# Splitting streamed weights in 128x1024 pieces in place of 128x512, in a kernel of 86 weight blocks

## What is computed

```python
h = rmsnorm(x, g_pre[i])
proj = h @ w_in[i]
qkv, z_a, b_raw, a_raw, glu_in, z_b, gate_logits = jnp.split(proj, _split_points(), axis=-1)
qkv = jax.nn.silu(causal_depthwise_conv(qkv, w_conv_qkv[i]))          # 4 taps
o_a = gated_delta_chunked(q, k, v, g_log, beta)                       # 16 heads
y_a = o_a @ w_br_a[i]
u = causal_depthwise_conv(jax.nn.glu(glu_in), w_dw[i]) + b_dw[i]      # 31 taps
u = jax.nn.silu(layernorm(u, ln_g[i], ln_b[i])) * jax.nn.silu(z_b)
y_b = u @ w_br_b[i]
mixed = (gate_a * y_a + gate_b * y_b) @ w_out[i]
```

## Time and profile before

| | |
|---|---|
| median of 3 runs | 2382.02 us |
| span of the profiled execution | 2380.3 us |
| TensorE products busy | 2285.8 us, 96% |
| VectorE busy | 1580.1 us, 66% |
| ScalarE busy | 1267.6 us, 53% |
| GpSimd busy | 195.4 us, 8% |
| low parts (L401) | 1376 instructions, 941.2 us |
| high parts (L395) | 1376 instructions, 839.7 us |

### The profile page before, as it was taken

One profiled execution on the slowest core, in us unless ns is written; L12 is line 12 of the kernel. 1 busy time (PEld: TensorE's weight loads), 2 busy tenths in 40 slices (PEclk: granted clock), 3 DMA queues, 4 the chain that ended last, 5 costly groups with the idle time before them and its releaser, 6 DMA issues.

```text
span 2380.3 us, 32496 instructions
## 1 busy us (share of the span) xinstructions
PE 2285.8 (96%) x10970; PEld 1869.3 (79%) x10970; DVE 1580.1 (66%) x2901; ACT 1267.6 (53%) x2513; POOL 195.4 (8%) x357
## 2 busy tenths in 40 slices
PE   6999999999999899899999999999999989999997
PEld 5788878788777777777888888788888868888885
DVE  4766666666699999987555556465366664456665
ACT  4555555555566666657444555455345445555542
POOL 0001010010123232220000000000000000000000
PEclk9999999999999999999999999999999999999998
DMA  6634343343456666654665656556555545654462
GB/s 202 177 107 125 106 118 111 106 123 107 120 154 166 186 176 169 165 189 161 236 204 189 237 197 204 198 182 208 150 191 172 200 143 181 194 177 130 153 212 89
DMA packets 400631, 393.47 MB, mean 165 GB/s; under 512 B 15296, under 2 KB 284624, under 8 KB 398992
## 3 DMA queue, kind: packets, MB, share of 16 engines
q1 hardware_dynamic: 395968, 369.57, 50.4%
q0 software_dynamic: 4272, 20.45, 2.6%
q10 hardware_dynamic: 288, 2.10, 0.2%
HBM read 387.85 MB, written 4.21 MB: 165 GB/s over the span
## 4 chain that ended last, share of the span: by engine, by line
PE 77%; DVE 13%; issue 6%; ACT 3%; DMA 1%; SPq 1%; DVEq 0%; POOL 0%; ACTq 0%; POOLq 0%
PE pair L423 20%; PE pair L421 20%; PE pair L422 20%; DVE acc L846 5%; DVE w_lo L401 3%; PE RA L623 2%; PE RB L635 2%; PE RB L633 2%; PE RA L1214 1%; PE QA L1199 1%; PE QA L479 1%; PE RB L627 1%; ACT w_hi L395 1%; ACT bth L774 1%; PE QA L759 0%
## 5 line engine op out<-in xcount | busy, mean ns | idle before, releaser
L401 DVE TENSOR_TENSOR w_lo<-raw,w_hi 128x512 fp32r<-128x512 f32 x1376 | 941.2, 697 | 443.5 <-ACT w_hi L395 443.1
L395 ACT ACTIVATE w_hi<-raw 128x512 fp32r<-128x512 f32 x1376 | 839.7, 628 | 489.5 <-PE pair L423 479.6
L421 PE MATMUL pair<-w_hi,in_hi 128*128 128x512 f32 x2368 | 981.7, 415 | 14.8 <-DVE w_lo L401 7.4
L423 PE MATMUL pair<-w_hi,in_lo 128*128 128x512 f32 x2368 | 930.9, 393 | 0.0
L422 PE MATMUL pair<-w_lo,in_hi 128*128 128x512 f32 x2368 | 928.2, 392 | 0.0
L421 PEld LDWEIGHTS pair<-w_hi,in_hi 128*128 128x128 f32 x2368 | 448.9, 190 | 102.8 <-DVE w_lo L401 9.5
L423 PEld LDWEIGHTS pair<-w_hi,in_lo 128*128 128x128 f32 x2368 | 447.3, 189 | 95.9
L422 PEld LDWEIGHTS pair<-w_lo,in_hi 128*128 128x128 f32 x2368 | 449.3, 190 | 83.5 <-issue 4.8
L846 DVE SCALAR_TENSOR_TENSOR acc<-upad,cwl,acc 128x256 f32<-128x256 f32 x336 | 187.3, 594 | 0.0
L667 ACT ACTIVATE tri<-RB 128x512 f32<-128x512 f32 x96 | 54.1, 563 | 145.7 <-PE RB L635 145.7
L715 DVE TENSOR_TENSOR xm<-RA,const 128x256 f32<-128x256 f32 x96 | 40.8, 425 | 76.8 <-PE RA L623 76.8
(11 more groups left out here) (370 smaller groups left out, 2106.1 us busy)
## 6 DMA issues: line engine op xcount, KB each, us to landing
raw<-in_w_in_dram SPq DMA_DIRECT2D x512, 256.0 KB, 3.6
raw<-in_w_in_dram SPq DMA_DIRECT2D x80, 1024.0 KB, 5.2
raw<-in_w_out_dram SPq DMA_DIRECT2D x48, 1024.0 KB, 5.0
raw<-in_w_kv_shared_dram SPq DMA_DIRECT2D x24, 1024.0 KB, 5.0
raw<-in_w_br_a_dram SPq DMA_DIRECT2D x16, 1024.0 KB, 5.1
raw<-in_w_br_b_dram SPq DMA_DIRECT2D x16, 1024.0 KB, 5.0
raw<-in_w_mem_kv_dram SPq DMA_DIRECT2D x16, 1024.0 KB, 4.9
raw<-in_w_ple_gate_dram SPq DMA_DIRECT2D x16, 1024.0 KB, 5.0
```

The source lines that it names most:

```text
L395: act.activation(w_hi[:, u % 2, q % UK], raw[:, u, q % UK], ACT.Copy).then_inc(hi_ready[u], 1)
L401: dve.tensor_tensor(w_lo[:, u % 2, q % UK], raw[:, u, q % UK], w_hi[:, u % 2, q % UK].bitcast(F32), ALU.subtract)\
L421: pe.matmul(o, xh, wh, start=(q == 0), stop=False)
L423: mm = pe.matmul(o, xl, wh, start=False, stop=(q == KC - 1))
```

## The change

High and low parts are made for two chunks at a time, on 128x1024, 688 instructions each in place of 1376. A pair is indexed by r = 0 to 7; three pairs are split ahead in place of six chunks. TensorE waits once for each pair. In the even lists ScalarE makes a pair ahead of `between` at hs 0, 4, 8, ... and VectorE after it at hs 1, 5, 9, ... In the lists for heads ScalarE makes its pair *after* `between`, at hs 0, 4, 9, 12, 16, 20, 24, 28, and VectorE at 3, 6, 10, 13, 18, 21, 25, 29. Cut to its core:

```diff
-AHEAD = 6
+PAIRS = KC // 2
+UP = UK // 2
+AHEAD = 3
@@ load_unit, load_heads
-        reach(sp, lo_ready[u], UK * blk)
+        reach(sp, lo_ready[u], UP * blk)
@@ hi_piece, lo_piece
+    def pair_of(x, r):
+
+        u, c = r // UP, r % UP
+        return x[:, u % x.shape[1], 2 * c:2 * c + 2].rearrange("p k n -> p (k n)")
+
-        if q == 2 * UK - 1:
+        if r == UP * 2 - 1:
             reach(act, psum_ready, blk)
-        elif q < 2 * UK:
-            reach(act, chunk_used, (KC - 1) * blk - (2 * UK - 2 - q))
+        elif r < 2 * UP:
+            reach(act, chunk_used, (KC - 1) * blk + 2 * r - 5)
         else:
-            reach(act, chunk_used, (KC - 1) * blk + q - 2 * UK + 1)
-        act.activation(w_hi[:, u % 2, q % UK], raw[:, u, q % UK], ACT.Copy).then_inc(hi_ready[u], 1)
+            reach(act, chunk_used, (KC - 1) * blk + 2 * (r - 2 * UP) + 2)
+        act.activation(pair_of(w_hi, r), pair_of(raw, r), ACT.Copy).then_inc(hi_ready[u], 1)
...
+        dve.wait_ge(hi_ready[u], UP * blk + r % UP + 1)
+        dve.tensor_tensor(pair_of(w_lo, r), pair_of(raw, r), pair_of(w_hi, r).bitcast(F32), ALU.subtract)\
            .then_inc(lo_ready[u], 1)
@@ pe_block
-            pe.wait_ge(lo_ready[u], UK * blk + q % UK + 1)
+            if q % 2 == 0:
+                pe.wait_ge(lo_ready[u], UP * blk + q % UK // 2 + 1)
@@ act_block, dve_block
+    HI_EVENLY, LO_EVENLY = tuple(range(0, 2 * KC, 4)), tuple(range(1, 2 * KC, 4))
+    HI_BESIDE_HEADS, LO_BESIDE_HEADS = (0, 4, 9, 12, 16, 20, 24, 28), (3, 6, 10, 13, 18, 21, 25, 29)
+
+    def act_block(act, blk, between=None, pieces_at=HI_EVENLY):
+        for hs in range(2 * KC):
+            first = pieces_at is HI_EVENLY
+            if between and not first:
+                between(hs)
+            if hs in pieces_at:
+                b, r = ahead(blk, pieces_at.index(hs))
+                if not isinstance(b, int) or b < BLK_END:
+                    hi_piece(act, b, r)
+            if between and first:
+                between(hs)
```

More of the change, by code:

```diff
@@ L381, in loads, with hi_piece, lo_piece, ahead @@
         return 64 * blk + 64
-    def hi_piece(act, blk, q):
-        u = q // UK
-        if q % UK == 0:
+    def pair_of(x, r):
+        u, c = r // UP, r % UP
+        return x[:, u % x.shape[1], 2 * c:2 * c + 2].rearrange("p k n -> p (k n)")
+    def hi_piece(act, blk, r):
+        u = r // UP
+        if r % UP == 0:
             act.wait_ge(w_loaded[u], loads(blk))
-        if q == 2 * UK - 1:
+        if r == UP * 2 - 1:
             reach(act, psum_ready, blk)
-        elif q < 2 * UK:
-            reach(act, chunk_used, (KC - 1) * blk - (2 * UK - 2 - q))
-        else:
-            reach(act, chunk_used, (KC - 1) * blk + q - 2 * UK + 1)
-        act.activation(w_hi[:, u % 2, q % UK], raw[:, u, q % UK], ACT.Copy).then_inc(hi_ready[u], 1)
[L397 to L401, removed]
+        elif r < 2 * UP:
+            reach(act, chunk_used, (KC - 1) * blk + 2 * r - 5)
+        else:
+            reach(act, chunk_used, (KC - 1) * blk + 2 * (r - 2 * UP) + 2)
+        act.activation(pair_of(w_hi, r), pair_of(raw, r), ACT.Copy).then_inc(hi_ready[u], 1)
+    def lo_piece(dve, blk, r):
+        u = r // UP
+        dve.wait_ge(hi_ready[u], UP * blk + r % UP + 1)
+        dve.tensor_tensor(pair_of(w_lo, r), pair_of(raw, r), pair_of(w_hi, r).bitcast(F32), ALU.subtract)\
            .then_inc(lo_ready[u], 1)
[L404 to L408, removed]
+    def ahead(blk, r):
+        if r + AHEAD < PAIRS:
+            return blk, r + AHEAD
+        return blk + 1, r + AHEAD - PAIRS
     def pe_block(pe, blk, parity, hi, lo, between=None):
@@ L429, in pe_block, with dve_block @@
                     between(2 * q + tile)
[L431 to L444, removed]
+    HI_EVENLY, LO_EVENLY = tuple(range(0, 2 * KC, 4)), tuple(range(1, 2 * KC, 4))
[11 more added lines that the diff above has]
+                between(hs)
+    def dve_block(dve, blk, between=None, pieces_after=LO_EVENLY):
         for hs in range(2 * KC):
@@ L448, in dve_block @@
             if hs in pieces_after:
-                b, p = ahead(blk, pieces_after.index(hs), 1)
+                b, r = ahead(blk, pieces_after.index(hs))
                 if not isinstance(b, int) or b < BLK_END:
-                    lo_piece(dve, b, p)
+                    lo_piece(dve, b, r)
     def keys_pe(pe, h, par, hs):
@@ L1893, in _ @@
         act_block(act, 1, beside([(keys, 0, 0)]))
-        heads = lambda h, i: act_block(act, h + i, beside([(rule, h + (i - 2), i), (keys, h + (i - 1), 1 - i)]))
+        heads = lambda h, i: act_block(act, h + i, beside([(rule, h + (i - 2), i), (keys, h + (i - 1), 1 - i)]), HI_BESIDE_HEADS)
         heads(2, 0)
@@ L1923, in _ @@
         dve_block(dve, 1, beside([(keys, 0, 0)]))
-        heads = lambda h, i: dve_block(dve, h + i, beside([(rule, h + (i - 2), i), (keys, h + (i - 1), 1 - i)]), BESIDE_HEADS)
+        heads = lambda h, i: dve_block(dve, h + i, beside([(rule, h + (i - 2), i), (keys, h + (i - 1), 1 - i)]), LO_BESIDE_HEADS)
         heads(2, 0)
```

## The result

The changed kernel takes 2403.12 us (median of 4 runs, 2402.38 to 2404.49) where the kernel before, run beside it, takes 2382.91 (2381.13 to 2384.28): 1.0082 times as long, 95% interval 1.0069 to 1.0094. That is 20.2 us slower; the forecast was 15.8 slower. Its profiled execution has a span of 2400.6 us, 20.3 more than the earlier trace rows.

What follows compares the result with a forecast made beforehand. TensorE was taken to bound heads and tail, VectorE the groups. Heads +24.6, groups -9.8 and start +1 give +15.8 us on a span of 2380.3, as a median 2397.8 us; 8 in 10 range 2384 to 2409.

Steps and rivals of the forecast that it cites:

- What bounds the kernel: TensorE bounds heads and tail, where shorter splits gain nothing; VectorE bounds the groups, where a cheaper split can pay.
- The heads' stalls: Blocks 2 to 15: low pairs waiting for high pairs behind `tri` delay `xm` by 0.88 us twice a block, +24.6 us.
- the gain at the start of the rule: Heads: VectorE has no piece at half-steps 31 and 1 any more, which can only help; counted 0.
- The groups: VectorE's rounds get 0.7 us shorter with pairs, -9.8 us over 14 rounds; bounds 0 and -27.3.
- The length of a round: Groups: a block takes about 24.3 us, with TensorE's waits near 1.4.
- TensorE's waits cover that: Groups: TensorE's waits, 2.1 us mean, cover the 0.7 us saved a round, so 14 rounds give -9.8.
- Rival (b): Heads stall, but groups gain nothing, as pairs bound to used chunks hold VectorE at more half-steps: 2407.6 us; chance 0.13.
- rival (c): Stalls in the heads make TensorE's clock fall there as in the groups, 8.6 us more: 2406.4 us; chance 0.08.
- The start: Block 1: TensorE's first product is behind one high and one low part, which grow by 0.95 us; taken as +1.
- The tail: Pairs are made in time on two half-idle engines: 0, between -2 and +2 us.
- the evictions behind a high pair in the groups: Groups: ScalarE's evictions of half-step 0 stand behind a high pair, but are covered by 1.1 us.
- blocks 16 to 18: Forecast 0; blocks 16 and 17 use the even list, with the high pair ahead of `tri`, so no stall.

Runs made afterwards that it cites:

- three experiments on order: Changed kernel, heads only: high pairs at half-steps 8 and 11, 2379.46 us; low pairs at 11 and 14, 2378.01; only the high pair of 9 moved to 8, 2390.95.
- Counted in chunks: Pairs everywhere, heads' high pairs at half-steps 8 and 11, each pair raising its counter by two: 2384.15 us, against 2379.46 for the same counted in pairs.
- the late list: Groups' low pairs at half-steps 1, 5, 11, 15, 19, 22, 25, 29, not 1, 5, 9, 13, 17, 21, 25, 29; alone in the changed kernel: 2394.79 us.
- the best version: Pairs in blocks 2 to 32 only, heads' high pairs at half-steps 8 and 11, groups' low pairs at 11, 15, 19, 22: 2368.64 us, ratio 0.9937.
- the kernel with single pieces at late places: The 2368.64 us kernel with each pair of the groups taken apart into two 128x512 pieces at the same queue place; heads keep pairs: 2378.41 us.
- the run with one late piece: Kernel before, one 512 piece per head in the changed order: high part behind `tri` at half-step 9, low part ahead of `xm` at 10: 2382.84 us.
- the three kernels with pairs at the late places: Groups' low pairs at half-steps 11, 15, 19, 22: pairs in blocks 2 to 32 only, 2368.64 us; in the changed kernel, 2394.79; with all orders mended, 2369.38.

## Why the prediction was right, and where it was off

**The range.** The measured 2403.12 us lies in the 8 in 10 range (2384 to 2409) and, by 0.1, outside the forecast's own (2392 to 2403).

**What bounds the kernel.** Right in the main: the tail gained nothing from the smaller work on VectorE, the groups did. The heads have a gain too, 3.3 us without the stalls, but by a place in the queue, as follows.

**The heads' stalls.** The mechanism and its size were right: `xm` 0.88 us late at half-steps 11 and 14 and nowhere else (block 11, half-step by half-step), 2.72 us from `tri` where the working had 2.71, the load's wait 1.13 where it had about 1.1, and the clock at 1.00. The three experiments on order confirm it from both engines and one stall at a time. What was mis-sized is the gain at the start of the rule, which was counted at 0 for want of a row: each block gets 0.24 us back there, so it takes 38.77 us, not 39.0, and the term is 14 x (1.76 - 0.24) = 21.3, against 24.6. In block 11 the first `xm` starts 1.94 us into the block in place of 2.19, and half-step 3 is 0.24 us earlier, with pairs counted either way: VectorE has no piece ahead of it at half-step 1 any more. Counted in chunks, about 0.08 of it is lost again at the hand-over ahead of `r` shown above.

**The groups.** The length of a round was right: 24.05 to 24.5 us without a fall, where 24.3 was forecast. But the rounds before averaged 24.91 over these 14 blocks (348.7 / 14), falls and all, and those of after 24.3 without what two falls cost ((342.8 - 2.4) / 14), so that 0.6 a round or 8.3 us is what the pairs saved, near the 9.8. The step that failed is the one behind it, "TensorE's waits cover that". It was worked out as if the falls of the clock stayed as harmless as they were; they were harmless because VectorE never waited for a high part that itself waited for a used chunk. A pair needs the later of its two chunks, and with that VectorE's round hangs on TensorE's: two falls left 1.2 us each. -8.3 + 2.4 = -5.9. Rival (b), that pairs bound to used chunks hold VectorE at more places, was half true, and through the clock; rival (c) looked for falls in the heads, where there are none, and missed that those in the groups would begin to count. The fall in block 33 (38.84 before, 40.64 after) is the +1.5 of that stretch; no step had it, and as another kernel's trace has it with the late list and two have not, part of it may be chance.

**The start.** +1.0 came as forecast: the first product of block 1 is at 59.56 in place of 58.6. A single trace could not have shown it, for this place varies by over a microsecond between traces (58.5 to 60.1 us in the six with single pieces there, 59.6 to 61.0 in the eight with pairs); the means are 59.1 and 60.1. It was given back within block 1, which waits later for other things: near 0 at block 2.

**The tail.** 2.7 against a bound of 2, and named nowhere: the prediction priced the evictions behind a high pair in the groups, and not in the tail, where the products of nine blocks wait for them.

The errors partly cancel: -3.4 in the heads, +3.9 in the groups, +4.2 in the tail and around block 33, -1.2 at the start and +0.9 in blocks 16 to 18 add, but for rounding, to the 4.5 us between 20.3 and 15.8. Their sizes add to 13.6 us, so that the total is no worse than this is in part luck; the direction rests on the heads' term, and that was understood.

## What to carry to other kernels

Joining two instructions makes each engine's work shorter and each chain longer: before doing it, go through the queue of every engine that makes or takes the larger tile, and ask for each place whether a short, awaited instruction stands behind it and whether its input is ready when its turn comes. Here two places of one half-step were worth 24 us, more than the best version gains over the kernel before (about 15). Give a joined instruction a place at which its input has long been made, or its saving goes into waits (11.7 us for one list here). An engine that sets the length of a round should wait for nobody: once its input is bound to another engine's progress, that engine's disturbances, which cost nothing before, are its own.

## What the runs showed of the hardware

A fall of TensorE's clock has no price of its own. In the groups each takes 3.4 us at the lower level, in every trace. It cost nothing in the kernel before (49.97 us for two rounds of 25.0) and in the kernel with single pieces at late places (26.45 + 22.95 = 49.40 for two of 24.7), and 1.2 us in the changed one. (A fall in the earliest of these rounds was not free even with single pieces: the run with one late piece, the same in the groups, has one in block 19, and blocks 19 and 20 take 49.7 us against 49.3 without it.) In these rounds falls came soon after a wait of TensorE of 1.9 to 2.6 us, in two to five of the 14; other waits as long had none behind them. In the three kernels with pairs at the late places, whose longest wait there was 1.8 us, there was no fall. In block 33 the same three kernels waited 2.4 us each, and one of them had a fall. That is what the traces have in common, not a cause that was tested.

A wait that is part of an instruction and one that stands ahead of it as an instruction of its own are not the same. With pairs that raise their counter by one, a waiting low pair starts 0.03 us after its high pair ends; with pairs that raise it by two, 0.10 us after. The 0.07 us are felt only where somebody waits for what follows: 0.07 us a block in the heads, 0.16 in a round of the groups, nothing in the tail's bare blocks (21.76 us both ways), and 4.7 us in the whole kernel (2384.15 against 2379.46), what differs by chance between executions, such as the number of falls, among them.
